# Weight products of the second expert stage moved from VectorE to GpSimd

## The chip, the cores and the metric

One NeuronCore of one Trainium2 chip runs the whole program. The metric is the device time of one execution in microseconds (us), the median of several runs. PE stands for TensorE, DVE for VectorE, ACT for ScalarE, POOL for GpSimd and SP for SyncE, the engine that issues most transfers. All data is float32; the large matrix products split each operand in a high part (fp32r) and a low remainder and use three matmuls.

## What is computed

The reference is one decoder layer for 512 tokens of width 2048: a combined projection, a gated convolution and differential attention, an output projection with layer norm, then a "product-key" expert layer, another norm and a gated embedding. Only the expert layer matters here:

```
q = (xb @ w_q).reshape(TOKEN_BLOCK, PEER_HEADS, 2, PEER_HALF)
s = einsum('thcd,hcnd->thcn', q, sub_keys)       # 128 keys per half, top 16 of each, top 16 of the sums
ids, g = ..., softmax(best)                      # 128 experts of 16384 per token
h = gelu(einsum('td,thkd->thk', xb, u_tab[ids]))
w = g * h
y = einsum('thk,thkd->td', w, v_tab[ids])        # x = LN(alpha * x + y)
```

## The kernel before

The tokens are split. For 352 tokens (`TU`) the expert layer is dense: the first expert stage computes gelu(u_tab x) for all 16384 experts, 128 units of 128 experts, and spills each 128x352 activation tile to HBM (`eg_sp[k, p, 0]`); the gates, summed per expert and token, are scattered into `eg_sp[k, p, 1]`, zero elsewhere. The second expert stage multiplies activation by gate and then by v_tab. The other 160 tokens are done sparsely: GpSimd gathers rows of u_tab and v_tab by indirect DMA (160 gathers of 128 rows of 2048 floats each, `NUP`), and VectorE does the dot products and, in the second stage, the weighted additions of rows.

The second expert stage is 16 groups of 8 K-chunks. In group g, TensorE runs 8 units u of two blocks each; a block is 8 chunks x 3 matmuls of 352 columns (`value_group`, L920, matmuls L651 to L653, called `three`). Its right-hand operands are the weights of the group: `xwhi[g % 2]` and `xwlo[g % 2]`, 8 tiles of 128x352 each, made one group ahead. Its left-hand operand is v_tab, streamed from HBM: SP loads `raw` (512 KB a block), ACT rounds it to `whi` (`hi_part`, L1019, L1025), and VectorE makes `wlo = raw - whi` (`lo_part`, L1575, L1578).

The weights of group g+1 are made during group g, tile k during unit k-1:

1. VectorE `weights_product` (L1651, instruction L1659): `wt = hg[.,0] * hg[.,1]`, activation times gate, 128x352. It waits for the transfer of `hg` (two chunks in 704 KB), and starts with a drain.
2. ACT `cast_weights` (L1234, L1237): `xwhi = fp32r(wt)`.
3. VectorE `weights_low` (L1661, L1664): `xwlo = wt - xwhi`.

VectorE's order in one unit (`add_values`, L1707) is: low part of tile u and product of tile u+1; wait for TensorE to have finished blocks 2u and 2u+1; add both banks to `res` (L1733 in group 0, L1735 after, 128x352 each, one input in PSUM); `lo_part` of block 2u+4; the gathered rows that fall in this unit (`add_early` L1683, `add_rows` L1675, instructions L1692, L1680: 128x2048, `y = row * w + y`, both tensors in SBUF); `lo_part` of block 2u+5. How many rows fall in a unit is written by hand in `V_ROWS`: group 0 has none, none, none, 1, 2, 2, 2, 2; group 1 has 1,1,1,2,1,2,1,2; groups 2, 3 and 14 have 1,2 four times; groups 4 to 13 have 1,1,1,2 twice; group 15 has 4 rows and no weights to make.

ACT's order in `value_steps` (L1239) is: `step(2u)`, which waits for block 2u and rounds the raw of block 2u+4; the cast of tile u+1; `step(2u+1)`, which rounds the raw of block 2u+5. So block 2u+5 is rounded after the cast, and the cast waits for the product of tile u+1:

```
for b in range(16):
    step(g * 16 + (B6 + b), b % 4)
    if b % 2 == 0 and not last:
        if b == 0: cast_weights(g + 1, 0, 1 - q)
        if b < 14: cast_weights(g + 1, b // 2 + 1, 1 - q)
```

SP's order in a group (`group_loads`, L510) is the raw of unit k, then, for odd k, a wait for the products up to tile k of the next group and the load of the `hg` pair that takes their place.

GpSimd, in this stage, only issues the row gathers (`gather_v`, L624, L631). There is a ring of 4 row buffers; gather n waits until VectorE has used row n-4. In the earlier part of the kernel (up to the first expert stage) and in its last part GpSimd makes the `wlo` instead of VectorE (L564, 128x1024); the same hardware pair can be seen at work there.

Of the kernel before, what the change touches and what calls it, by code (L numbers as in the profile page):

```python
# [19 lines left out]
F32 = mybir.dt.float32  # L20
F32R = mybir.dt.float32r
U32 = mybir.dt.uint32
ALU = mybir.AluOpType
# [33 lines left out]
B6 = B5 + 2 * U5  # L57
# [23 lines left out]
RING = 4  # L81

NXP = NP // NJ
NUP = NXP + NP


V_ROWS = [(0, 0, 0, 1, 2, 2, 2, 2), (1, 1, 1, 2, 1, 2, 1, 2), (1, 2, 1, 2, 1, 2, 1, 2), (1, 2, 1, 2, 1, 2, 1, 2),
          (1, 1, 1, 2, 1, 1, 1, 2), (1, 2, 1, 2, 1, 2, 1, 2), (1, 1, 1, 1, 0, 0, 0, 0)]
V_EARLY, V_LOOPED, V_EVE, V_LAST = 4, 4, 5, 6
# [3 lines left out]
V_START += [V_START[V_EVE] + sum(V_ROWS[V_EVE])]  # L93
assert V_START[V_LAST] + sum(V_ROWS[V_LAST]) == NUP
assert V_START[V_LOOPED] % 4 == 0 and 2 * V_PER % 4 == 0 and V_START[V_EARLY - 1] >= NXP
NTG = 24
TILE_DOTS = [j % 4 != 3 for j in range(32)]
POST_DOTS = [j % 5 != 4 and j < 20 for j in range(4 * (64 - POST))]
assert sum(TILE_DOTS) == NTG and NTG * NRT + sum(POST_DOTS) == NUP and NTG % RING == 0
assert NTG < NXP <= 2 * NTG  # L100

# [19 lines left out]
def build(nc, ws, xT, pT, cpar, pvec, lamT, keysT, u_tab, v_tab, out):  # L121
# [6 lines left out]
    with ExitStack() as ctx:  # L128
# [38 lines left out]
        xwhi = [at(f"xwhi{i}", o, [P, 8, TU], F32R) for i, o in enumerate((o_s, o_ahi))]  # L167
        xwlo = [at(f"xwlo{i}", o + 12 * KB, [P, 8, TU], F32R) for i, o in enumerate((o_s, o_ahi))]
# [7 lines left out]
        def small(name, shape, dt=F32):  # L176
            n = 4
            for s in shape[1:]:
                n *= s
            t = at(name, c[0], shape, dt)  # L180
            c[0] += (n + 31) // 32 * 32
            return t
# [113 lines left out]
        hg = small("hg", [P, 2, 2, 2, TU])  # L296
        wt = small("wt", [P, 2, TU])
# [30 lines left out]
        blk_done = sem("blk_done")  # L328
# [51 lines left out]
        hg_first = [sem(f"hg_first{i}") for i in range(2)]  # L380
        hg_in = [sem(f"hg_in{i}") for i in range(2)]
# [19 lines left out]
        wt_ok = sem("wt_ok")  # L401
        cast_ok = sem("cast_ok")
        w_ok = sem("w_ok")
# [136 lines left out]
        def _(pool):  # L540
# [80 lines left out]
                    pool.dma_start(hg[:, n % 2], eg_sp[2 * n:2 * n + 2].rearrange("k p c t -> p k c t")  # L621
                                   ).then_inc(hg_first[n % 2], 16)

            def gather_v():  # L624

                pool.wait_ge(blk_done, B6)
                for n in range(NUP):
                    if n >= RING:
                        pool.wait_ge(rows_used, NUP + n - RING + 1)
                    at_col = xg[:, 0, n:n + 1].bitcast(U32) if n < NXP else idx[:, n - NXP:n - NXP + 1]  # L630
                    nc.gpsimd.indirect_dma_start(  # L631
                        vrows[:, n % RING], None, v_tab,
                        bass.IndirectOffsetOnAxis(ap=at_col, axis=0)).then_inc(rows_in[n % RING], 16)
# [4 lines left out]
            pool.wait_ge(xg_in, 16 * NJ)  # L638
            gather_u()
            first_gates()  # L640
            gather_v()

            pool.wait_ge(lo_done, B7)
            lo_parts(B7, NB - B7)
# [673 lines left out]
        def _(dve):  # L1318
# [14 lines left out]
            for q in range(KD // 2):  # L1333
                k = slice(2 * q, 2 * q + 2)
# [209 lines left out]
            last = TT - 1  # L1544
# [64 lines left out]
            def expert_tile(t, extra=False):  # L1609
                n = 0  # L1610

                def next_dot():
                    nonlocal n
                    if extra and NTG * t + n < NXP:
                        extra_dot(NTG * t + n)
                    else:
                        dot(NTG * t + (n - NXP), NTG // RING * t + n // RING, n % RING)
                    n += 1
# [19 lines left out]
            for t in range(3, NRT):  # L1638
                expert_tile(t)
            n = NTG * NRT  # L1640
            for j, with_dot in enumerate(POST_DOTS):
# [6 lines left out]
            dve.drain().then_inc(dots_ok, 1)  # L1648


            def weights_product(g, k, ahead=False):  # L1651

                s = k // 2 % 2
                dve.drain()
                if ahead:
                    dve.wait_ge(hg_first[s], g * 32 + 16 * (k // 4 + 1))
                else:
                    dve.wait_ge(hg_in[s], g * 32 + 16 * (k // 4 - 2))
                dve.tensor_tensor(wt[:, k % 2], hg[:, s, k % 2, 0], hg[:, s, k % 2, 1], ALU.mult).then_inc(wt_ok, 1)  # L1659

            def weights_low(g, k, q):  # L1661

                dve.wait_ge(cast_ok, g * 8 + (k - 7))
                dve.tensor_tensor(xwlo[q][:, k], wt[:, k % 2], xwhi[q][:, k].bitcast(F32), ALU.subtract  # L1664
                                  ).then_inc(w_ok, 1)

            def weights_here(k):
                weights_product(0, k, ahead=True)
                dve.drain()
                dve.tensor_copy(xwhi[0][:, k], wt[:, k % 2])  # L1670
                dve.drain()
                dve.tensor_tensor(xwlo[0][:, k], wt[:, k % 2], xwhi[0][:, k].bitcast(F32), ALU.subtract
                                  ).then_inc(w_ok, 1)
# [33 lines left out]
            def add_values(g, q, kind, i=0):  # L1707
                first, eve, last = kind == 0, kind == V_EVE, kind == V_LAST
                if eve:
                    dve.wait_ge(yx_full, 1)  # L1710
                    r = res[:, :, TU:TD]
                    dve.scalar_tensor_tensor(r, r, ALPHA, quad[:, 0:KD * NX].rearrange("p (k t) -> p k t", k=KD),
                                             ALU.mult, ALU.add)
                    dve.drain().then_inc(yx_used, 1)
                for u in range(8):
                    ahead = not last or u < 6
                    if not last:

                        if u == 0:
                            weights_product(g + 1, 0, ahead=first)  # L1720
                        if u == 1:
                            weights_low(g + 1, 0, 1 - q)
                        if u >= 1:
                            weights_low(g + 1, u, 1 - q)
                        if u < 7:
                            weights_product(g + 1, u + 1, ahead=first and u < 3)
                    dve.wait_ge(blk_done, g * 16 + (B6 + 2 * u + 2))
                    for n in range(2):
                        r = res[:, 2 * u + n, 0:TU]
                        p = ps[2 * ((u + 1) % 2) + n][:, 0:TU]  # L1730
                        if first:

                            ad = dve.scalar_tensor_tensor(r, r, ALPHA, p, ALU.mult, ALU.add)  # L1733
                        else:
                            ad = dve.tensor_tensor(r, r, p, ALU.add)  # L1735
                    ad.then_inc(evac6, 1)
                    if ahead:
                        lo_part(g * 16 + (B6 + 2 * u + 4), 2 * u % 4)
                    if last:
                        for n in range(2):  # L1740
                            dve.drain()
                            if u == 0 and n == 0:
                                dve.tensor_copy(msum2[:, 0:TU], res[:, 0, 0:TU])
                            else:
                                dve.tensor_tensor(msum2[:, 0:TU], msum2[:, 0:TU], res[:, 2 * u + n, 0:TU], ALU.add)
                    start = V_START[kind] + sum(V_ROWS[kind][:u])
                    for r in range(start, start + V_ROWS[kind][u]):
                        if kind < V_EARLY:
                            add_early(r)
                        elif kind == V_LOOPED:  # L1750
                            r += q * V_PER
                            add_rows(2 * V_PER * i + r, V_PER // 2 * i + r // RING, r % RING)
                        else:
                            add_rows(r, r // RING, r % RING)
                    if last and u == 3:
                        dve.drain().then_inc(yacc_ok, 1)
                    if last and u == 4:
                        dve.wait_ge(p_in, 16)
                        dve.tensor_copy(phi[:], pin[:])
                        dve.drain()  # L1760
                        dve.tensor_tensor(plo[:], pin[:], phi[:].bitcast(F32), ALU.subtract).then_inc(p_ok, 1)
                    if last and u == 6:

                        dve.wait_ge(yacc_full, 1)
                        for n in range(4):
                            r = res[:, 4 * n:4 * n + 4, TD:T]
                            dve.scalar_tensor_tensor(r, r, ALPHA, ps[4 + n][:].rearrange("p (k t) -> p k t", k=4),
                                                     ALU.mult, ALU.add)
                        dve.drain().then_inc(yacc_used, 1)
                        dve.tensor_reduce(msum2[:, TU:T], res[:, :, TU:T].rearrange("p k t -> p t k"), AX.X, ALU.add)  # L1770
                    if ahead:
                        lo_part(g * 16 + (B6 + 2 * u + 5), (2 * u + 1) % 4)
# [79 lines left out]
```

## Time and profile before

| | |
|---|---|
| three runs | 3876.55, 3867.3, 3873.48 us |
| median | 3873.48 us |
| span of the profiled execution | 3703.5 us (its own device time is not listed beside it) |
| PE busy | 3634.4 us, 98% |
| DVE busy | 2612.3 us, 71% |
| ACT busy | 1289.2 us, 35% |
| POOL busy | 1692.4 us, 46% |
| second expert stage | from 2476 us to 3464 us of the span |

The span runs from the first to the last instruction; the device time has some 170 us more around it (3873.48 - 3703.5). Shares of busy time are means over stages that differ; the second expert stage is a quarter of the span, and is read by itself below. A "low part" below is an L1578 instruction, a "row" an L1680 or L1692 instruction.

### The profile page before, as it was taken

The numbers are of one execution on the slowest core, as the hardware profiler recorded it, in microseconds if no ns is written. First come the engines' busy times: TensorE is split into PE (matmuls) and PEld (weight loads), VectorE is DVE, ScalarE is ACT, GpSimd is POOL, SyncE is SP. The second block draws the span as 40 slices with busy tenths as digits, with TensorE's granted clock in tenths as the row PEclk, the third lists the DMA queues.
The fourth block names the chain that finished last, engine by engine and source line by source line (L and its number), as shares of the span: only waits on it lengthen the run. The fifth ranks groups of instructions, "written<-read, shape, count | busy, mean of one in ns | idle before, by whom it ended". The sixth has DMA issues, their size and how long they took to land.

```text
span 3703.5 us, 56572 instructions
## 1 busy us (share of the span) xinstructions
PE 3634.4 (98%) x19704; PEld 3304.0 (89%) x19704; DVE 2612.3 (71%) x4018; ACT 1289.2 (35%) x1659; POOL 1692.4 (46%) x1044
## 2 busy tenths in 40 slices
PE   8999999999999899999999999999999999999999
PEld 6888888877888688999999999989999999999777
DVE  3555555553431499987889888779999999999732
ACT  4334433343121523344433333323333333333532
POOL 4444444433444244668777776633332222222143
PEclk9999999999999999999999999999999999999999
DMA  5343333333443223478999999999999999999232
GB/s 182 128 131 125 130 125 130 128 106 117 151 135 124 77 87 101 158 274 304 340 369 376 367 372 363 325 340 352 381 372 356 358 359 352 361 357 343 86 117 76
DMA packets 245798, 873.52 MB, mean 236 GB/s; under 512 B 35600, under 2 KB 76752, under 8 KB 204624
## 3 DMA queue, kind: packets, MB, share of 16 engines
q1 hardware_dynamic: 154864, 496.64, 38.6%
q0 software_dynamic: 59360, 340.13, 23.9%
q10 hardware_dynamic: 31488, 35.66, 2.7%
q8 instruction: 47, 0.77, 0.1%
q14 instruction: 39, 0.32, 0.0%
HBM read 813.38 MB, written 58.90 MB: 236 GB/s over the span
## 4 chain that ended last, share of the span: by engine, by line
PE 63%; POOL 16%; DVE 10%; issue 5%; DMA 2%; DVEq 2%; ACT 1%; ACTq 0%; SPq 0%; POOLq 0%
PE bank L651 20%; PE bank L653 20%; PE bank L652 20%; POOL expert_spill L587 12%; POOL urows L605 4%; DVE hot L1524 1%; PE quad L694 1%; DMA expert_spill<-gval,goff 1%; DVE sc L1387 1%; PE bank L713 1%; DVE pick L1527 1%; DVE topi L1488 0%; DVE topi L1481 0%; DVE s4b L1482 0%; DMA urows<-u_tab,idx 0%
## 5 line engine op out<-in xcount | busy, mean ns | idle before, releaser
L1025 ACT ACTIVATE whi<-raw 128x1024 fp32r<-128x1024 f32 x784 | 827.9, 1059 | 1944.7 <-PE bank L653 1340.3
L651 PE MATMUL bank<-ahi,whi 128*128 128x352 f32 (+1 forms) x3968 | 1430.7, 361 | 44.0 <-DVE wlo L1578 22.7
L653 PE MATMUL bank<-ahi,wlo 128*128 128x352 f32 (+1 forms) x3968 | 1416.6, 357 | 0.0
L652 PE MATMUL bank<-alo,whi 128*128 128x352 f32 (+1 forms) x3968 | 1416.0, 357 | 0.0
L564 POOL TENSOR_TENSOR wlo<-raw,whi 128x1024 fp32r<-128x1024 f32 x316 | 787.7, 2496 | 1070.8 <-ACT whi L1025 1058.1
L651 PEld LDWEIGHTS bank<-ahi,whi 128*128 128x128 f32 x3968 | 750.7, 189 | 139.9 <-issue 30.9
L653 PEld LDWEIGHTS bank<-ahi,wlo 128*128 128x128 f32 x3968 | 750.8, 189 | 76.9
L652 PEld LDWEIGHTS bank<-alo,whi 128*128 128x128 f32 x3968 | 751.1, 189 | 72.3 <-issue 0.5
L651 PE MATMUL bank<-xwhi,whi 128*128 128x352 f32 x2048 | 662.7, 324 | 3.1 <-issue 1.7
L653 PE MATMUL bank<-xwhi,wlo 128*128 128x352 f32 x2048 | 658.6, 322 | 0.0
L652 PE MATMUL bank<-xwlo,whi 128*128 128x352 f32 x2048 | 658.0, 321 | 0.0
L1578 DVE TENSOR_TENSOR wlo<-raw,whi 128x1024 fp32r<-128x1024 f32 x472 | 575.6, 1220 | 18.3 <-ACT whi L1025 15.9
L587 POOL DMA_INDIRECT expert_spill<-gval,goff x384 | 449.1, 1170 | 145.6 <-issue 115.5
L631 POOL DMA_INDIRECT vrows<-v_tab,idx x128 | 207.0, 1617 | 547.6 <-DVE yacc L1680 492.0
L651 PEld LDWEIGHTS bank<-xwhi,whi 128*128 128x128 f32 x2048 | 385.4, 188 | 4.2 <-issue 1.9
L652 PEld LDWEIGHTS bank<-xwlo,whi 128*128 128x128 f32 x2048 | 386.6, 189 | 0.0
L653 PEld LDWEIGHTS bank<-xwhi,wlo 128*128 128x128 f32 x2048 | 385.0, 188 | 0.0
L1584 DVE SCALAR_TENSOR_TENSOR urows<-urows,quad 128x2048 f32<-128x2048 f32 x128 | 292.6, 2286 | 70.0 <-DMA urows<-u_tab,idx 69.0
L1680 DVE SCALAR_TENSOR_TENSOR yacc<-vrows,hd,yacc 128x2048 f32<-128x2048 f32 x116 | 273.4, 2357 | 24.9 <-issue 23.5
L1387 DVE SCALAR_TENSOR_TENSOR sc<-glu,cur,sc 128x512 f32<-128x512 f32 x232 | 270.2, 1165 | 17.3
L1237 ACT ACTIVATE xwhi<-wt 128x352 fp32r<-128x352 f32 x120 | 59.8, 498 | 345.0 <-DVE wt L1659 343.1
L1353 DVE RECIPROCAL rcp<-sums 128x2 f32<-128x2 f32 x32 | 5.3, 166 | 230.8 <-ACTq L1084 230.8
(229 smaller groups left out, 2787.8 us busy)
## 6 DMA issues: line engine op xcount, KB each, us to landing
raw<-ws SPq DMA_DIRECT2D x788, 512.0 KB
hg<-expert_spill SPq DMA_DIRECT2D x58, 704.0 KB, 9.1
expert_spill<-zero SPq DMA_DIRECT2D x32, 704.0 KB, 5.9
expert_spill<-hst ACTq DMA_DIRECT2D x128, 176.0 KB
gate_spill<-gout ACTq DMA_DIRECT2D x32, 256.0 KB, 2.0
gl<-gate_spill SPq DMA_DIRECT2D x32, 256.0 KB, 2.7
expert_spill<-gval,goff POOLq DMA_INDIRECT x384
hg<-expert_spill POOLq DMA_DIRECT2D x6, 704.0 KB, 6.1
```

What stands on the lines that cost most here:

```text
L564: nc.gpsimd.tensor_tensor(wlo[:, s], raw[:, s // 2, s % 2], whi[:, s].bitcast(F32), ALU.subtract).then_inc(lo_done, 1)
L587: nc.gpsimd.indirect_dma_start(eg_flat, bass.IndirectOffsetOnAxis(ap=goff[here, a, n:n + 1], axis=0), gval[here, a, n:n + 1], None).then_i ...
L605: nc.gpsimd.indirect_dma_start(urows[:, n % RING], None, u_tab, bass.IndirectOffsetOnAxis(ap=at_col, axis=0)).then_inc(rows_in[n % RING], 16)
L631: nc.gpsimd.indirect_dma_start(vrows[:, n % RING], None, v_tab, bass.IndirectOffsetOnAxis(ap=at_col, axis=0)).then_inc(rows_in[n % RING], 16)
L651: pe.matmul(ps_out, hi, xh, start=first, stop=False)
L652: pe.matmul(ps_out, hi, xl, start=False, stop=False)
L653: return pe.matmul(ps_out, lo, xh, start=False, stop=last)
L1025: act.activation(whi[:, s], raw[:, s // 2, s % 2], ACT.Copy).then_inc(hi_done, 1)
L1387: dve.scalar_tensor_tensor(dst, glu[:, w:w + T], cur[:, w:w + 1], acc, ALU.mult, ALU.add)
L1578: dve.tensor_tensor(wlo[:, s], raw[:, s // 2, s % 2], whi[:, s].bitcast(F32), ALU.subtract).then_inc(lo_done, 1)
L1584: dve.scalar_tensor_tensor(urows[:, s], urows[:, s], 1.0, quad[:], ALU.mult, ALU.mult, accum_out=hd[:, bass.ds(n, 1)]).then_inc(rows_used, 1)
L1680: dve.scalar_tensor_tensor(yacc[:], vrows[:, s], w, yacc[:], ALU.mult, ALU.add).then_inc(rows_used, 1)
```

## The change

GpSimd makes the products and their low halves for groups 1 to 15 (120 products and 120 low parts of 128x352). For group 0 VectorE still makes them, as before (`weights_here`). GpSimd's `gather_v` is cut in pieces: the first four gathers, and then for each unit those gathers whose buffer is freed by a row of that unit. Ahead of each piece come the low part of tile u and the product of tile u+1 of the next group. ACT's casts and SP's loads keep their order and their waits.

```diff
@@ gpsimd
-            def gather_v():
-                pool.wait_ge(blk_done, B6)
+            def weights_product(g, k):
+                s = k // 2 % 2
+                pool.drain()
+                if g == 1 and k < 4:
+                    pool.wait_ge(hg_first[s], g * 32 + 16 * (k // 4 + 1))
+                else:
+                    pool.wait_ge(hg_in[s], g * 32 + 16 * (k // 4 - 2))
+                nc.gpsimd.tensor_tensor(wt[:, k % 2], hg[:, s, k % 2, 0], hg[:, s, k % 2, 1], ALU.mult
+                                        ).then_inc(wt_ok, 1)
+            def weights_low(g, k):
+                pool.wait_ge(cast_ok, g * 8 + (k - 7))
+                nc.gpsimd.tensor_tensor(xwlo[g % 2][:, k], wt[:, k % 2], xwhi[g % 2][:, k].bitcast(F32),
+                                        ALU.subtract).then_inc(w_ok, 1)
+            def gather_v(unit):
                 for n in range(NUP):
+                    if n >= RING and ROW_UNIT[n - RING] != unit or n < RING and unit >= 0:
+                        continue
                     if n >= RING:
                         pool.wait_ge(rows_used, NUP + n - RING + 1)
...
-            gather_v()
+            pool.wait_ge(blk_done, B6)
+            gather_v(-1)
+            pool.wait_ge(w_ok, 8)
+            for g in range(16):
+                for u in range(8):
+                    if g < 15:
+                        if u == 0:
+                            weights_product(g + 1, 0)
+                        if u == 1:
+                            weights_low(g + 1, 0)
+                        if u >= 1:
+                            weights_low(g + 1, u)
+                        if u < 7:
+                            weights_product(g + 1, u + 1)
+                    gather_v(8 * g + u)
@@ vector, add_values
-                    if not last:
-                        if u == 0:
-                            weights_product(g + 1, 0, ahead=first)
-                        if u == 1:
-                            weights_low(g + 1, 0, 1 - q)
-                        if u >= 1:
-                            weights_low(g + 1, u, 1 - q)
-                        if u < 7:
-                            weights_product(g + 1, u + 1, ahead=first and u < 3)
                     dve.wait_ge(blk_done, g * 16 + (B6 + 2 * u + 2))
```

## Rows read from the trace of the kernel before

**Rows 1.** Windows: time, then busy us (and instructions) of each engine, clock, DMA
```profile
2602.00:2662.00 60.00, 60.00 (x374) 60.00 (x374) 58.25 (x59) 19.34 (x24) 23.37 (x12) 1.00 0.98 383
2980.00:3040.00 60.00, 60.00 (x379) 60.00 (x378) 55.50 (x58) 19.91 (x24) 14.63 (x10) 1.00 0.96 358
```

**Rows 2.** Waits of PE in the second expert stage, 2476 to 3464 us
```profile
PE bank L651 <- issue: 1.7, 1, 1.7
PE bank L651 <- DVE xwlo L1664: 0.6, 1, 0.6
```

**Rows 3.** Chain of waits, start us, us, what; second expert stage, its longest pieces
```profile
2542.59 0.43 PE bank L651
2725.19 3.49 PE quad L949 x32
2729.53 0.29 PE bank L652
```

**Rows 4.** Lines of DVE from 2476 to 3464 us, busy, mean ns, idle before
```profile
L1659 DVE TENSOR_TENSOR wt<-hg 128x352 f32<-128x352 f32 x122 | 64.1, 525 | 13.0 <-issue 3.7
L1664 DVE TENSOR_TENSOR xwlo<-wt,xwhi 128x352 fp32r<-128x352 f32 x120 | 61.0, 519 | 0.0
L1733 DVE SCALAR_TENSOR_TENSOR res<-res,bank 128x352 f32<-128x352 f32 x16 | 7.6, 517 | 9.5 <-PE bank L653 9.5
```

**Rows 5.** Timeline of DVE, start us and duration, one unit with one row
```profile
2869.45 0.94 DVE L1735 TENSOR_TENSOR res<-res,bank 128x352 f32<-128x352 f32 x2
2870.31 1.22 DVE L1578 TENSOR_TENSOR wlo<-raw,whi 128x1024 fp32r<-128x1024 f32 x1
2871.74 2.35 DVE L1680 SCALAR_TENSOR_TENSOR yacc<-vrows,hd,yacc 128x2048 f32<-128x2048 f32 x1 [0.21 <-issue]
2874.01 1.22 DVE L1578 TENSOR_TENSOR wlo<-raw,whi 128x1024 fp32r<-128x1024 f32 x1
2875.14 0.52 DVE L1664 TENSOR_TENSOR xwlo<-wt,xwhi 128x352 fp32r<-128x352 f32 x1
2875.75 0.53 DVE L1659 TENSOR_TENSOR wt<-hg 128x352 f32<-128x352 f32 x1
2876.20 0.95 DVE L1735 TENSOR_TENSOR res<-res,bank 128x352 f32<-128x352 f32 x2
```

**Rows 6.** Timeline of DVE, two rows in one unit (x2)
```profile
2544.98 4.80 DVE L1692 SCALAR_TENSOR_TENSOR yx<-vrows,hx,yx 128x2048 f32<-128x2048 f32 x2 [0.45 <-issue]
```

**Rows 7.** Timeline of POOL: gathers in a unit with one row, then with two
```profile
2874.36 1.68 POOL L631 DMA_INDIRECT vrows<-v_tab,idx  x1 [5.50 <-DVE yacc L1680]
...
2547.60 3.00 POOL L631 DMA_INDIRECT vrows<-v_tab,xg  x1 [4.26 <-DVE yx L1692]
2550.90 0.94 POOL L631 DMA_INDIRECT vrows<-v_tab,xg  x1 [0.30 <-issue]
```

**Rows 8.** Line L564 up to 1620 us: POOL's own subtraction, min/median/max ns
```profile
L564 POOL TENSOR_TENSOR wlo<-raw,whi x280: 2346/2401/3217, 7.6 to 1595.2; 128x1024 fp32r<-128x1024 f32 x140
```

**Rows 9.** Line L1387 of DVE, two SBUF inputs: min/median/max ns; one POOL instruction beside it
```profile
L1387 DVE SCALAR_TENSOR_TENSOR sc<-glu,cur,sc x232: 750/752/2834, 92.9 to 795.2; 128x512 f32<-128x512 f32 x116
...
308.57 2.40 POOL L564 TENSOR_TENSOR wlo<-raw,whi 128x1024 fp32r<-128x1024 f32 x1 [2.92 <-ACT whi L1025]
308.76 2.76 DVE L1387 SCALAR_TENSOR_TENSOR sc<-glu,cur,sc 128x512 f32<-128x512 f32 x1
```

**Rows 10.** Timeline at 1308 us: DVE with one SBUF input beside a POOL subtraction
```profile
1308.09 2.40 POOL L564 TENSOR_TENSOR wlo<-raw,whi 128x1024 fp32r<-128x1024 f32 x1 [3.98 <-ACT whi L1025]
...
1308.51 0.42 DVE L1481 FIND_INDEX8 pnow<-bnow,cand 128x8 uint32<-128x256 f32 x1
```

**Rows 11.** Timeline of ACT around 2876 us
```profile
2876.31 0.50 ACT L1237 ACTIVATE xwhi<-wt 128x352 fp32r<-128x352 f32 x1 [2.75 <-DVE wt L1659]
2876.72 1.04 ACT L1025 ACTIVATE whi<-raw 128x1024 fp32r<-128x1024 f32 x1
```

**Rows 12.** Waits of the SP queue, 2740 to 3360 us: us in total, times, longest
```profile
SPq L500 <- DVE wt L1659: 23.0, 40, 1.6
```

More of the change, by code:

```diff
@@ L95 @@
 assert V_START[V_LOOPED] % 4 == 0 and 2 * V_PER % 4 == 0 and V_START[V_EARLY - 1] >= NXP
+V_UNITS = [V_ROWS[g] if g < V_LOOPED else V_ROWS[V_LOOPED] for g in range(14)] + [V_ROWS[V_EVE], V_ROWS[V_LAST]]
+ROW_UNIT = [8 * g + u for g in range(16) for u in range(8) for _ in range(V_UNITS[g][u])]
+assert len(ROW_UNIT) == NUP
 NTG = 24
@@ L1648, in _, with weights_here @@
             dve.drain().then_inc(dots_ok, 1)
-            def weights_product(g, k, ahead=False):
+            def weights_here(k):
                 s = k // 2 % 2
                 dve.drain()
[L1655 to L1658, printed above, removed]
+                dve.wait_ge(hg_first[s], 16 * (k // 4 + 1))
                 dve.tensor_tensor(wt[:, k % 2], hg[:, s, k % 2, 0], hg[:, s, k % 2, 1], ALU.mult).then_inc(wt_ok, 1)
[L1661 to L1668, printed above, removed]
                 dve.drain()
```

## The prediction

> **What bounds the kernel now.** I read the page first: PE is busy 98% of the span. Then the windows of the second expert stage [rows 1]: PE is busy all of the 60 us, in groups 1 to 3 (first row) as in the looped groups (second row). The counts of the second row give the pace: 379 matmuls less the one that straddles the edge, so 60 / 378 = 0.159 us a matmul, 3.81 us a block of 24, 7.62 us a unit of two blocks. The waits of PE say how much the change could give [rows 2]: 0.6 us on a low half of the weights, in a stage of 988 us; the chain shows the place, 2542.59 us, the start of group 1 [rows 3]. The pace in groups 1 to 3 is 374 instead of 379 matmuls in 60 us, 1.3%, over 180 us some 2.4 us. That VectorE's load causes it is not shown; if it does, the most to be had is 0.6 + 2.4, say 3 us, under 0.1%. The second bound lies close behind: DVE is busy 58.25 of 60 us in groups 1 to 3 and 55.50 in the loop [rows 1]. So the question is not what PE gains, but whether DVE stays ahead of PE.
>
> **What is removed.** From DVE, 120 products of 0.525 us and 120 low parts of 0.519 us [rows 4], 125 us. A unit with one row takes 2876.20 - 2869.45 = 6.75 us, and 2875.14 - 2869.45 = 5.69 us of it is without the weights [rows 5]: 1.06 us a unit go. A second row adds 2.45 us [rows 6]. Without the weights a one-row unit takes 5.69 us and a two-row unit 8.14 us; the loop (six and two in a group) means 6.30 us, groups with 1,2,1,2 mean 6.92 us. Against 7.62 us both are faster than PE, if nothing is added.
>
> **What is added on POOL.** Its subtraction of 1024 columns takes 2.40 us [rows 8]; in proportion 352 columns take 0.83 us, an estimate without the fixed part of an instruction. Two of these and 1.25 gathers of 1.68 to 3.00 us [rows 7] are at most 5.4 us in a unit of 7.62: POOL has the time, and its own busy time costs nothing. What costs is where its work falls, in two ways.
>
> **First term: VectorE and GpSimd exclude each other.** Ahead of the first stage a DVE instruction with two inputs in SBUF takes 0.75 us, but 2.76 us when it begins 0.19 us after a POOL subtraction of 2.40 us [rows 9]: it is held up 2.01 us, so POOL holds it off for 2.20 of its 2.40 us. An instruction with one input in SBUF, beside the same POOL instruction, keeps its 0.42 us [rows 10]. In the second stage the low parts and the rows have two SBUF inputs, and the bank additions one. The POOL instruction of 0.83 us would hold off a low part or a row by up to 0.83 - 0.20 = 0.63 us (an estimate), and in turn waits for one that runs. Two of them, 1.26 us, are more than the 1.06 us that were removed. The Trainium skill, page SBUF — State Buffer, section Who interferes with whom, says that a VectorE instruction with two SBUF inputs and a GpSimd instruction that reads SBUF exclude each other, the later one blocked until the earlier is through. By the whole instruction, 0.83 us, one hold-off in each of the 117 units with rows would be 0.20 us longer, and the sum 23 us higher, 3945 us; this trace has 2.20 of 2.40, and the sum goes by the trace.
>
> **Second term: the order on POOL and ACT.** I walk one unit, W = 0 at its first bank addition, with DVE late (not waiting for PE). From [rows 5]: first low part 0.86 to 2.08, row 2.29 to 4.64, second low part to 5.77, next W at 5.69. The gather behind a row starts 0.27 us after the row and takes 1.68 [rows 7]; with 0.30 of issue, POOL asks for its low half 2.25 us after the row's end, which is W + 1.20. The first low part is already running since 0.86. So:
> - Late case: POOL's low half runs 2.08 to 2.91, the row ends at 5.06, and the product, asked for meanwhile, runs 5.06 to 5.89. The cast waits for the product, and block 2u+5 is rounded behind the cast: 1.48 us from the product's end to the end of that rounding [rows 5, 11]. The second low part begins at 7.42; next W at 8.55.
> - Early case (the low half was made under the bank additions): product 2.08 to 2.91, row to 5.06, next W at 6.11.
> After a late unit the gather ends some 7.1 us after W and the low half comes under the next bank additions, so that the next unit is an early one; after an early or a two-row unit a late one follows (the second gather of a pair ends 2.06 us after the second row [rows 6, 7], so the low half is asked for at W + 1.31). A two-row unit in the early case takes 6.11 + 2.45 = 8.56 us; in the late case the product holds the second row off for 0.54 more, 9.1 us.
>
> **The sum.** Loop, rows 1,1,1,2: 8.55 + 6.11 + 8.55 + 8.56 = 31.77 against 4 x 7.62 = 30.48 us, 1.29 us in four units, 20 times: 26 us. Pairs 1,2: 17.11 against 15.24, 1.87 us; groups 2, 3 and 14 have four, 22.4 us; group 1 has 1.29 + 2 x 1.87 = 5 us. Group 0 with its four two-row units: 0.94 + 3 x 1.48 = 5.4 us. Together 59 us. Off go two credits: in group 0 DVE waited 9.5 us for PE [rows 4], a lead of which I take half, 5 us; and PE's pause of 3.49 us with 12 matmuls at half its clock behind it, 0.29 instead of 0.16 us each (one of them stands in [rows 3]), 5 us in which DVE catches up. 49 us remain. Against the span of 3703.5 us that is 3752.5; its own device time is not shown, so I add it to the median: 3873.5 + 49 = **3922 us**.
>
> **Bounds of this.** Below: if POOL's instructions always find the gap, every unit is an early one (6.11 and 8.56, means 6.72 and 7.34, both under 7.62), and the cost is none, the gain up to 3 us. Above: every unit is a late one: the loop 6 x 8.55 + 2 x 9.1 = 69.5 against 61 us, 85 us in ten groups; groups 2, 3 and 14 9.6 us each, group 1 9, group 0 5; less 10: 118 us. I take the walk between them, since it follows the instants of the rows.
>
> **Edits that I cost at nothing.** The first four gathers stay where they were; the first two products come behind them, some 4 x 1.68 = 6.7 us later, and with them ACT's rounding of block 5. PE needs block 5 five blocks, 19 us, after the stage's start, and tile 0 of group 1 after 61 us; both hide it. The added drains on POOL have nothing but the previous low half to wait for. SP waits for the odd products before the hg load and has the next raw load behind it: before, 23 us in 40 waits, 0.6 each [rows 12]. Where the product comes at 5.89, and the first low part is done by 2.08, the raw load starts 3.8 us later; I add nothing, since four raw buffers stand ahead of that load, and keep it for the upper end.
>
> **Rivals.**
> 1. Not slower: the DVE time freed makes it wait for PE, W comes later against the gather, POOL's low half falls into that wait and the product costs 0.42 us (5.06 - 4.64). It decides at 0.35 us of wait in a one-row unit (1.20 - 0.86). For it: the DVE is then under PE's 7.62 us everywhere. Against it: every two-row unit (8.56) costs the wait again, and groups 1 to 3 begin with DVE late. 3870 to 3881 us. Chance 0.24.
> 2. Only the hold-offs, and no late rounding: 1.26 - 1.06 = 0.20 us a unit more than before where DVE was saturated (32 units), 6 us, and part of the loop: 3881 to 3898 us. Chance 0.13.
> 3. Much slower: all late, raw loads held behind SP's wait, and PE's clock at the lower level after each long stall, as at 2729 us [rows 3] (1.6 us each time): above 3963 us, up to 3991. Chance 0.15.
> 4. Faster by more than 8 us: nothing in PE's waits holds that much; 0.03.
> The forecast, 3898 to 3963 us, has 0.45.
>
> **Numbers.** A measurement of this kernel can tell about 0.2% (8 us) from no change. Slower is 0.45 + 0.13 + 0.15 = 0.73, same 0.24, faster 0.03. The range of 8 in 10 takes in rival 1 nearly whole and most of rival 3: 3868 to 3985 us; the forecast's own range is 3898 to 3963.
>
> **What would show it.** DVE's low parts and rows longer than 1.22 and 2.35 us on the mean, by about 0.6 us where a POOL instruction lies ahead; L1578 waiting for ACT's whi, and PE waiting for DVE's wlo, in groups 1 to 3 above all; products of POOL beginning at the end of a row rather than ahead of it; PE's pace in the loop above 7.62 us a unit. I am wrong in the mechanism if rows and low parts keep their lengths; wrong in the size, if PE still shows no waits in the loop, where the first term alone is too small. A POOL instruction of 352 columns far from 0.83 us would move both terms.

## The result, and the profile after

The changed kernel takes 4188.6 us (median of 4 runs, 4182 to 4199), the kernel before 3875.0 us beside it (4 runs, 3867 to 3887): a ratio of 1.081, 95% interval 1.079 to 1.084. That is 314 us slower. The forecast was slower, by 49 us, with a range up to 3985 us; the time lies 204 us above that range.

The first look is at the page, the chain of waits by engine, and a window of 600 us from the looped groups of the second expert stage (for the kernel before, see the looped row of [rows 1]).

```profile
PE 3813.8 (91%) x19704; PEld 3417.6 (81%) x19704; DVE 2555.1 (61%) x3778; ACT 1274.5 (30%) x1659; POOL 1887.5 (45%) x1284
...
PE 52%; issue 21%; POOL 11%; DVE 9%; POOLq 3%; DVEq 2%; ACT 1%; DMA 1%; ACTq 0%; SPq 0%
...
3060.00:3660.00 600.00, 505.84 (x2875) 489.87 (x2874) 395.75 (x315) 143.98 (x179) 223.15 (x193) 0.93 0.74 271
```

PE was busy for all of a 60 us window in the looped groups; now it is busy 506 of 600 us, and that time holds only 2875 matmuls, 0.176 us each instead of 0.159, at a granted clock of 0.93 instead of 1.00. But DVE is not what is full in its place: 396 of 600 us, 66%, where [rows 1] had 55.50 of 60. Nor is POOL, with 223 of 600. Every engine waits, which is the look of a chain of waits and not of a bound engine. The waits of the same stretch name its links:

```profile
ACT xwhi L1272 <- POOL wt L635: 415.0, 59, 11.2
POOL wt L635 <- issue: 305.5, 59, 7.5
DVE wlo L1613 <- ACT whi L1060: 188.6, 51, 7.3
PE bank L686 <- DVE wlo L1613: 93.8, 46, 6.5
```

From the bottom up: PE waits for VectorE's low parts, these for ACT's rounding, ACT's cast for POOL's product (L635), and the product for "issue", for nothing that the profile counts as work. 305.5 us in 59 times are 5.2 us each. What stands on POOL's queue there is the drain ahead of the product, L630 (minimum, median and maximum in ns), and the timeline of POOL in two units shows where it lies:

```profile
L630 POOLq DRAIN  x120: 1027/8260/19903, 2651.7 to 3883.7; - x120
```

```profile
2966.57 0.97 POOL L652 DMA_INDIRECT vrows<-v_tab,idx  x1
2967.84 0.94 POOL L652 DMA_INDIRECT vrows<-v_tab,idx  x1 [0.30 <-issue]
2968.79 1.18 POOL L641 TENSOR_TENSOR xwlo<-wt,xwhi 128x352 fp32r<-128x352 f32 x1
2975.95 0.94 POOL L635 TENSOR_TENSOR wt<-hg 128x352 f32<-128x352 f32 x1 [5.98 <-issue]
2977.05 0.96 POOL L652 DMA_INDIRECT vrows<-v_tab,idx  x1 [0.16 <-issue]
2978.02 0.94 POOL L641 TENSOR_TENSOR xwlo<-wt,xwhi 128x352 fp32r<-128x352 f32 x1
```

The low half ends at 2969.97 and the product begins at 2975.95. Between them POOL does nothing but drain. The drain's own record is longer, 8.26 us in the median, since it begins on the queue while the gather and the low half ahead of it still run; what it adds in idle time of POOL is the 5.2 us. The prediction had it at nothing.

One thing did not fit. The profiled span is 494 us longer than that of the kernel before (4197.3 - 3703.5), and the median time only 314 us. The windows of the first expert stage, which the change doesn't touch, from its first block to the first of the second stage, before and after:

```profile
1451.00:2476.00 1025.00, 1000.62 (x6180) 994.74 (x6179) 863.75 (x1578) 367.81 (x424) 729.85 (x590) 0.99 0.87 319
```

```profile
1448.00:2647.00 1199.00, 1083.50 (x6179) 1039.35 (x6178) 865.90 (x1580) 365.44 (x422) 723.98 (x590) 0.93 0.78 273
```

The first stage is 174 us longer, at 273 instead of 319 GB/s. The kernel before has 170 us between its listed times (3873) and its span (3703.5), while the changed kernel's own device time, 4199.2 us, is its span and 2 us. So the profile of before seems to be of an execution some 170 us faster than the runs listed beside it. The experiments below take that up.

### The profile page after: what moved, and what is told of

Its sections match the earlier page's. It is cut to its first block, busy times and chain, and to the rows that moved or that the text cites. A ratio compares the mean times of both kernels' runs of the same rounds, so it can differ in the third digit from the quotient of the medians.

```text
span 4197.3 us, 56477 instructions
## 1 busy us (share of the span) xinstructions
PE 3813.8 (91%) x19704; PEld 3417.6 (81%) x19704; DVE 2555.1 (61%) x3778; ACT 1274.5 (30%) x1659; POOL 1887.5 (45%) x1284
## 4 chain that ended last, share of the span: by engine, by line
PE 52%; issue 21%; POOL 11%; DVE 9%; POOLq 3%; DVEq 2%; ACT 1%; DMA 1%; ACTq 0%; SPq 0%
PE bank L686 16%; PE bank L688 16%; PE bank L687 16%; POOL wt L635 4%; POOLq L630 3%; POOL vrows L652 3%; POOL expert_spill L590 2%; DVE hot L1559 1%; POOL xwlo L641 1%; PE quad L729 1%; POOL urows L608 1%; DVE sc L1422 1%; DVE wlo L1613 1%; PE bank L748 1%; DVE yacc L1702 1%
## 5 line engine op out<-in xcount | busy, mean ns | idle before, releaser
L1613 DVE TENSOR_TENSOR wlo<-raw,whi 128x1024 fp32r<-128x1024 f32 x472 | 623.6, 1322 | 665.3 <-ACT whi L1060 584.8
L686 PE MATMUL bank<-xwhi,whi 128*128 128x352 f32 x2048 | 706.9, 345 | 223.7 <-DVE wlo L1613 209.5
L687 PE MATMUL bank<-xwlo,whi 128*128 128x352 f32 x2048 | 689.2, 337 | 0.0
L688 PE MATMUL bank<-xwhi,wlo 128*128 128x352 f32 x2048 | 688.4, 336 | 0.0
L686 PEld LDWEIGHTS bank<-xwhi,whi 128*128 128x128 f32 x2048 | 411.5, 201 | 253.3 <-DVE wlo L1613 235.3
L590 POOL DMA_INDIRECT expert_spill<-gval,goff x384 | 420.8, 1096 | 141.1 <-issue 115.5
L635 POOL TENSOR_TENSOR wt<-hg 128x352 f32<-128x352 f32 x120 | 175.2, 1460 | 644.1 <-issue 644.1
L687 PEld LDWEIGHTS bank<-xwlo,whi 128*128 128x128 f32 x2048 | 413.1, 202 | 0.0
L688 PEld LDWEIGHTS bank<-xwhi,wlo 128*128 128x128 f32 x2048 | 411.3, 201 | 0.0
L608 POOL DMA_INDIRECT urows<-u_tab,idx x128 | 157.0, 1227 | 218.6 <-DVE urows L1619 186.2
```

The lines of the kernel that those rows point to most:

```text
L590: nc.gpsimd.indirect_dma_start(eg_flat, bass.IndirectOffsetOnAxis(ap=goff[here, a, n:n + 1], axis=0), gval[here, a, n:n + 1], None).then_i ...
L608: nc.gpsimd.indirect_dma_start(urows[:, n % RING], None, u_tab, bass.IndirectOffsetOnAxis(ap=at_col, axis=0)).then_inc(rows_in[n % RING], 16)
L635: nc.gpsimd.tensor_tensor(wt[:, k % 2], hg[:, s, k % 2, 0], hg[:, s, k % 2, 1], ALU.mult).then_inc(wt_ok, 1)
L686: pe.matmul(ps_out, hi, xh, start=first, stop=False)
L687: pe.matmul(ps_out, hi, xl, start=False, stop=False)
L688: return pe.matmul(ps_out, lo, xh, start=False, stop=last)
```

## The experiments

All other comparisons ran beside runs of the kernel before of 3708 or 3709 us in the median, not 3873. "The drainless kernel" below is the change with its drain replaced as in the first experiment. Stage times below are from the first matmul of the stage to the first one behind it. In the profile of before the second expert stage takes 988.2 us, and a looped group 61.0 us (median).

**A semaphore in place of the drain.** The drain guards one thing: the product overwrites a buffer that the low half two tiles earlier has read. A wait for the count of finished low halves does the same.

```diff
@@ gpsimd, weights_product
-                pool.drain()
+                pool.wait_ge(w_ok, g * 8 + k - 1)
```

> The changed kernel with the one drain ahead of each GpSimd product replaced by a wait for the count of finished low halves (the reader of the buffer that the product overwrites). Everything else stays. Theory A (the drain waits for the row gathers in flight, 7 us and more a unit, and ACT's cast and rounding wait behind it): nearly all of the 313 us go; what is left is what GpSimd's work costs by itself. Theory B (mutual exclusion of VectorE and GpSimd and the late rounding, the two terms of the prediction, are the main cost): the time stays above 4100 us. If A holds, this run also measures the prediction's two terms: 3898 to 3963 us if they were right, under 3885 us if GpSimd's instructions find the gaps.

3776.6 us against 3708.8, ratio 1.018 (1.016 to 1.020): 68 us over the kernel before. The second stage takes 1058 us. Theory A stands, and the run also measures what the prediction had costed: 68 us where 49 stood.

**The drains alone.** The products and low halves stay on VectorE.

```diff
@@ gpsimd, on the kernel before (gather_v is cut in pieces as in the change)
-            gather_v()
+            pool.wait_ge(blk_done, B6)
+            gather_v(-1)
+            pool.wait_ge(w_ok, 8)
+            for g in range(16):
+                for u in range(8):
+                    if g < 15:
+                        if u == 0:
+                            pool.drain()
+                        if u < 7:
+                            pool.drain()
+                    gather_v(8 * g + u)
```

> The kernel before, with its products and low halves on VectorE, the gathers cut in the same pieces as in the change, and one GpSimd drain where the change has one, with nothing of the weights on GpSimd. Theory A: each drain takes about as long as in the change (5 to 10 us behind a gather, 1 us where none is in flight), the gathers come at most once in some 9.5 us, VectorE waits for rows, and the time is 4050 to 4250 us. Theory B: drains have nothing to wait for, within 10 us of the kernel before.

3901.8 us, one run: 193 us over the kernel before, with none of the weights' arithmetic on GpSimd. The 105 drains of units 0 to 6 (in unit 0 the second one) have a median like the change's (ns); the short ones, 34 to 53 ns, come right behind another drain. The 15 first drains of unit 0 are not in the line; their median is 15.99 us.

```profile
L654 POOLq DRAIN  x105: 34/8159/12242, 2503.8 to 3594.5; - x105
```

The expectation was 4050 to 4250 us on a base of 3873; on this base that is 3885 to 4085, and the run lies at its lower end. Here the rows come late and VectorE waits for them, and ACT's cast waits for VectorE's product (469.4 us in 72 times from 2740 to 3500 us) and not for one of GpSimd.

**The change again, on the same base.**

> The changed kernel as it is, so that it stands on the same chip as the experiments. In the first comparison the kernel before took 3873 us, beside the experiments it took 3709 us, and its profile spanned 3703.5 us. The first expert stage, which the change does not touch, took 1199 us in the profile of the changed kernel and 1025 us in that of the kernel before. If that is the chip or its memory and not the change, the first stage takes about 1027 us here too, and the time is 3709 + 196 (drains alone) + 68 (without drains) = 3973 us or up to 60 more if the two add to more than their sum (the second stage took 1312 us in the profile against 988). If the change itself slows the first stage, it takes some 1199 us here and the time is above 4150 us.

4030.7 us against 3707.7, ratio 1.086 (1.083 to 1.090), 323 us slower. The first stage takes 1024 us, as in the kernel before: what was 174 us longer in the first comparison is not the change. The second takes 1316 us, as in the first profile of the change (1312). So the second stage holds the whole cost, 328 us of it. The parts, 193 and 68 us, make 261; 62 us more are left. That they come from both standing in one line (the drain, the product behind it and the gather behind that are in series) is argued, and no run shows it. The window of the stage shows in what form PE pays:

```profile
2473.00:3789.00 1316.00, 1088.12 (x6193) 1058.72 (x6193) 850.78 (x699) 305.23 (x376) 477.41 (x404) 0.92 0.72 263
```

PE is idle for 228 us of it, where it was idle for 2 us before; and its matmuls, as many as before, take 1088 us instead of 986, with the granted clock at 0.92 instead of 1.00. So about 226 us of the 328 are idle time and 102 us are slower matmuls.

**Short rows.** The change, with a quarter of the bytes in each gather. It leaves out three quarters of each row, so its result is not that of the kernel.

```diff
@@ gpsimd, gather_v
-                        vrows[:, n % RING], None, v_tab,
+                        vrows[:, n % RING, 0:512], None, v_tab.rearrange("e (q d) -> (e q) d", q=4),
@@ gpsimd
+            nc.gpsimd.memset(vrows[:], 0.0)
+            pool.drain()
             gather_v(-1)
```

> The change with its drains, but each gather of values brings 512 columns a row (from another place of the table) instead of 2048; the rest of each row buffer is set to zero once, and the values of the last 160 tokens are left wrong by that. As many rows and descriptors, a quarter of the bytes. If the drain waits for the landing of the gathers in flight, the drains behind one gather fall from some 8 us to 3.5 to 5.5 us, and the second stage to 1030 to 1130 us. If it waits for GpSimd's own making of the descriptors, they keep their 8 us and the stage its length.

3841.1 us, one run; the second stage takes 1122 us. The drains, first of the change again, then with short rows:

```profile
L630 POOLq DRAIN  x120: 1025/8257/19727, 2478.1 to 3713.9; - x120
```

```profile
L630 POOLq DRAIN  x120: 1031/5236/7505, 2493.4 to 3529.8; - x120
```

A gather still has 128 rows, and the median drain falls from 8.26 to 5.24 us. But not only the bytes fall: the trace has 64 packets of 4 KB a gather here, and 128 of 8 KB in the change, so this run alone doesn't tell the bytes from the count of packets. The times of the packets say it more sharply. Between 2700 and 3700 us of the span I took each drain of over 2 us and the last packet of the last gather issued before its end: the drain ends 0.42 us (median; 0.37 to 0.58) behind that packet's end in the change, 0.47 (0.36 to 0.57) with short rows, and 0.43 (0.36 to 0.67) in the kernel with the drains alone, 253 drains in all. In these kernels a GpSimd drain waits until the row gathers that GpSimd has issued have landed.

**Only the products, and only the low halves.** Both without the drain: the product waits for the count of finished low halves, on VectorE too in the second kernel.

```diff
@@ gpsimd, only the products            @@ gpsimd, only the low halves
-  weights_low(g + 1, 0)                -  weights_product(g + 1, 0)
-  weights_low(g + 1, u)                -  weights_product(g + 1, u + 1)
@@ vector, add_values (as before)       @@ vector, add_values (as before)
+  weights_low(g + 1, 0, 1 - q)         +  weights_product(g + 1, 0, ahead=first)
+  weights_low(g + 1, u, 1 - q)         +  weights_product(g + 1, u + 1, ahead=first and u < 3)
```

> Without the drain, only the products on GpSimd, the low halves back on VectorE. The product is the part on which ACT's cast and the rounding of block 2u+5 wait. If the prediction's second term (late product, late rounding) is what remains without the drain, this has most of what the drainless kernel has over the kernel before; if the exclusion by count of instructions is, about half of it. If nothing remains in the drainless kernel, it is within 8 us of the kernel before.

> Without the drain, only the low halves on GpSimd, the products back on VectorE. Nothing of ACT waits on GpSimd here. By the second term nothing remains: within 8 us of the kernel before. By the exclusion alone, 0.63 us lost for 0.52 removed a unit, also within 8 us, perhaps 10 slower.

Products only: 3713.6 us, ratio 1.0013 (1.0002 to 1.0023), 5 us slower. Low halves only: 3717.6 us, ratio 1.0027 (1.0011 to 1.0043), 9 us slower. Together they cost 68. So neither the product's place in ACT's order nor a cost in proportion to the count of instructions explains it, and the next two runs go at the order itself.

**The order of ACT, and of POOL.**

```diff
@@ scalar, value_steps
-                    if b % 2 == 0 and not last:
+                    if b % 2 == 1 and not last:
-                        if b == 0:
+                        if b == 1:
                             cast_weights(g + 1, 0, 1 - q)
-                        if b < 14:
+                        if b < 15:
                             cast_weights(g + 1, b // 2 + 1, 1 - q)
```

> Without the drain, and with ACT's cast of tile u+1 placed behind step(2u+1) instead of behind step(2u), so that the rounding of block 2u+5 does not wait for the product. If the late rounding (second term) makes the 68 us that the drainless kernel has over the kernel before, at most 15 us of them stay: by the walk 6.11 to 6.85 us a one-row unit and 8.56 a two-row unit, 3705 to 3725 us. If the exclusion is the cause, over 40 us of the 68 stay.

3772.4 us, ratio 1.017 (1.014 to 1.020): 65 us over the kernel before, so of the 68 us nearly all stay. The late rounding is not the cause.

```diff
@@ gpsimd
                        if u == 1:
                            weights_low(g + 1, 0)
+                       if u < 7:
+                           weights_product(g + 1, u + 1)
                        if u >= 1:
                            weights_low(g + 1, u)
-                       if u < 7:
-                           weights_product(g + 1, u + 1)
```

> Without the drain, with GpSimd making the product of tile u+1 ahead of the low half of tile u, so that the product comes 0.95 us earlier and is never pushed behind the row. Both instructions still exclude VectorE. If the late product is the cause, the time falls to 3705 to 3725 us; if the exclusion is, it stays within 15 us of the drainless kernel's 3777 us.

3764.3 us, ratio 1.015 (1.012 to 1.018), 57 us slower, 12 us under the drainless kernel. The exclusion is left. These are VectorE's lines in the drainless kernel, 2740 to 3400 us:

```profile
L1613 DVE TENSOR_TENSOR wlo<-raw,whi 128x1024 fp32r<-128x1024 f32 x162 | 340.8, 2104 | 2.3 <-ACT whi L1060 2.3
L1702 DVE SCALAR_TENSOR_TENSOR yacc<-vrows,hd,yacc 128x2048 f32<-128x2048 f32 x97 | 229.1, 2362 | 22.9 <-issue 22.9
L1747 DVE TENSOR_TENSOR res<-res,bank 128x352 f32<-128x352 f32 x162 | 76.4, 513 | 0.0
```

A low part took 1.22 us in [rows 5] and takes 2.10 us on the mean now; the rows keep their 2.36 us, and the bank additions wait for PE no more. Where the time goes, the timelines of POOL and of DVE show:

```profile
2963.65 1.71 POOL L652 DMA_INDIRECT vrows<-v_tab,idx  x1 [3.92 <-DVE yacc L1702]
2965.38 1.86 POOL L641 TENSOR_TENSOR xwlo<-wt,xwhi 128x352 fp32r<-128x352 f32 x2
2967.21 0.93 POOL L635 TENSOR_TENSOR wt<-hg 128x352 f32<-128x352 f32 x1
```

```profile
2964.43 0.94 DVE L1747 TENSOR_TENSOR res<-res,bank 128x352 f32<-128x352 f32 x2
2965.29 3.93 DVE L1613 TENSOR_TENSOR wlo<-raw,whi 128x1024 fp32r<-128x1024 f32 x1
2969.43 2.35 DVE L1702 SCALAR_TENSOR_TENSOR yacc<-vrows,hd,yacc 128x2048 f32<-128x2048 f32 x1 [0.20 <-issue]
```

The gather ends just as VectorE's bank additions do (2965.36 and 2965.37), and POOL's instructions, back to back, then get through ahead of the first low part: here three (tile 0 and 1 of a group's beginning), 3.93 us for 1.22, otherwise mostly two. The low part does not get in between them, although its record begins 0.09 us ahead of POOL's first. Over the 660 us, 81 low parts lie beside POOL's arithmetic and 81 do not: these keep a median of 1.22 us, and the others take 2.12 us beside one instruction (12 times), 3.02 beside two (59) and 3.93 beside three (10), 0.90 us for each.

For products only, the same line over the same stretch shows what a single instruction does:

```profile
L1603 DVE TENSOR_TENSOR wlo<-raw,whi 128x1024 fp32r<-128x1024 f32 x171 | 240.9, 1409 | 0.0
```

0.19 us more a low part, 0.38 a unit, since only 37 of POOL's 81 us in this stretch lie beside low parts; 35 lie beside the bank additions, which have one SBUF input and keep their 0.515 us. In the drainless kernel it is 0.885 a low part, 1.77 us a unit: 150 of POOL's 154 us lie beside low parts. Against the 1.06 us removed [rows 5] a single one is a loss of nothing (0.38 for 0.52), and two are a loss of 0.71 us a unit. VectorE had less than that to spare in the loop: 6.75 us a one-row unit and 9.20 a two-row unit mean 7.36 against PE's 7.62.

**Writes only.** GpSimd's instructions stay in number, place and semaphores, but read nothing; the weights of groups 1 to 15 are not computed. The fills are also shorter, 0.41 us instead of 0.95.

```diff
@@ gpsimd, weights_product and weights_low of the drainless kernel
-                nc.gpsimd.tensor_tensor(wt[:, k % 2], hg[:, s, k % 2, 0], hg[:, s, k % 2, 1], ALU.mult
-                                        ).then_inc(wt_ok, 1)
+                nc.gpsimd.memset(wt[:, k % 2], 0.01).then_inc(wt_ok, 1)
...
-                nc.gpsimd.tensor_tensor(xwlo[g % 2][:, k], wt[:, k % 2], xwhi[g % 2][:, k].bitcast(F32),
-                                        ALU.subtract).then_inc(w_ok, 1)
+                nc.gpsimd.memset(xwlo[g % 2][:, k].bitcast(F32), 0.0).then_inc(w_ok, 1)
```

> The drainless kernel, with each of GpSimd's products and low halves replaced by a fill of the same 128x352 tile with a constant, which reads nothing from SBUF (so the weights of groups 1 to 15 are not computed). Same count, same places, same semaphores; the fill of 352 columns took 0.39 us at the kernel's start, the product 0.95. If VectorE is held off because GpSimd reads SBUF, its low parts keep their 1.22 us and a looped group takes 61 to 62 us. If any GpSimd instruction beside it holds it off, the low parts grow by up to 0.8 us a unit (0.4 each on the mean), still within what VectorE has, so that it is the length of the low parts and not the time that tells.

3700.2 us, one run, beside one of 3709.3 of the kernel before. The lines of DVE and POOL, 2740 to 3400 us:

```profile
L1611 DVE TENSOR_TENSOR wlo<-raw,whi 128x1024 fp32r<-128x1024 f32 x174 | 211.7, 1217 | 0.0
...
L1745 DVE TENSOR_TENSOR res<-res,bank 128x352 f32<-128x352 f32 x174 | 82.6, 515 | 100.8 <-PE bank L686 100.7
```

```profile
L640 POOL MEMSET xwlo<- 128x352 f32 x88 | 35.0, 407 | 0.1
L635 POOL MEMSET wt<- 128x352 f32 x86 | 34.3, 408 | 0.0
```

The low parts are back at 1.217 us, and VectorE waits 101 us for PE. Most of the 174 fills lie beside bank additions or idle time and test nothing, but 47 of them ran wholly within a low part (24 low parts), and those took 1.21 us too. One of them, VectorE and then GpSimd:

```profile
2949.88 1.21 DVE L1611 TENSOR_TENSOR wlo<-raw,whi 128x1024 fp32r<-128x1024 f32 x1
...
2949.90 0.41 POOL L640 MEMSET xwlo<- 128x352 f32 x1
2950.23 0.41 POOL L635 MEMSET wt<- 128x352 f32 x1
```

It is GpSimd's reading that holds VectorE off. The Trainium skill, page SBUF — State Buffer, section Who interferes with whom, says that a GpSimd instruction which only writes doesn't contend with a VectorE instruction of two SBUF inputs; this run agrees, and so do the 2.10 us of the drainless kernel with what it says of one that reads. This kernel is also the bound of what the move could have given, since here VectorE is rid of the work at no price: the second stage takes 984.5 us against 988.2, 3.7 us.

## Why the prediction was wrong

**The limit of the gain was right.** The prediction had "say 3 us" as the most to be had; the kernel with the work gone and no price gains 3.7 us in the stage.

**The step that failed is the drain.** "The added drains on POOL have nothing but the previous low half to wait for." They wait for the landing of the row gathers: of 120 drains 102 take over 2 us, and the median of all is 8.26 us. The gather was in the trace with its landing, 6.2 to 10.4 us after issue, and each product was put behind one; what a drain on a queue with transfers in flight does was not in any row, and the term should have been bounded from both sides, above by that landing, and not set at nothing. A one-row unit then is drain, product, gather, landing in series, 9.80 us in the change again (2969.17 to 2978.97 from product to product), against the 7.62 of PE:

```profile
2969.17 0.95 POOL L635 TENSOR_TENSOR wt<-hg 128x352 f32<-128x352 f32 x1 [7.13 <-issue]
2970.27 0.96 POOL L652 DMA_INDIRECT vrows<-v_tab,idx  x1
2971.25 0.94 POOL L641 TENSOR_TENSOR xwlo<-wt,xwhi 128x352 fp32r<-128x352 f32 x1
2978.97 0.95 POOL L635 TENSOR_TENSOR wt<-hg 128x352 f32<-128x352 f32 x1 [6.78 <-issue]
```

Over 112 units 2.2 us each would be 244 us, and units with two rows take one gather more. Replacing the drain takes away 254 of the 323 us (4030.7 to 3776.6 us).

**The first term, exclusion, was right in kind and too small.** It was set at 0.63 us for a POOL instruction and found to be 0.885 on the mean of all units, 0.90 for each that lies beside a low part. A POOL instruction of 352 columns takes 0.95 us, not the 0.83 of proportion: (2.40 - 0.95) / 672 columns is 2.16 ns a column, which leaves 0.19 us that don't depend on the columns. And its place was off: I let 0.30 us of issue pass between gather and low half, so that VectorE's low part came first; it is 0.02 us (2965.36 to 2965.38), and POOL gets through first. The walk also let a row be held off, but the rows kept their 2.36 us: it is the first low part that pays. By rows it is then 1.77 - 1.06 = 0.71 us a unit more than VectorE had before; by the 7.36 us above that is 8.07 us a unit, 64.6 us a group. The looped groups took 65.5 us (median) instead of 61.0.

**The second term, the late rounding, was wrong.** It would have been gone with ACT's other order, and 65 us of the 68 stayed. In the drainless kernel the product comes ahead of the row, not behind it. That the walk's 49 us came near the 68 is luck, two errors against each other.

**The rivals.** Without the drain the kernel is the second rival in kind, only the hold-offs and no late rounding; that rival's cost, up to 25 us, was too small. The third, much slower, had raw loads and PE's clock for its causes. The granted clock was at the lower level for 207 us of the second stage in the change again, against 3 us before, and in the drainless kernel for only 24: it follows the long waits. 161 us of PE's busy time lie at that level, and by the 0.29 us of a matmul there against 0.16 some 70 of the 102 us of slower matmuls are the clock's, an estimate. What the 328 us would have been at the full clock is open, since PE would have waited longer for POOL where it was faster; the 254 us of the drain's replacement hold the clock's part with the rest.

**The base.** The median was taken from listed runs of 3873 us and the sums from a span of 3703.5; the difference was called time around the span. It is 2 us. The change's first profile has the rest in the first stage (1199 against 1025 us, 273 against 319 GB/s), and the kernel before seems to have had it too: the change costs 314 us on the one base and 323 on the other. Why the first stage was slower there, by the chip, its memory or something else, is not shown; no trace of the kernel before at 3873 us is at hand.

## What to carry to other kernels

A GpSimd drain behind gathers that GpSimd issued is a wait for their landing; where it guards a buffer, a wait on the reader's semaphore can take its place, and here it brought back 254 us. Work moved to GpSimd is not free for VectorE if it reads SBUF: one instruction a unit, partly beside VectorE's PSUM additions, cost 5 or 9 us in all, two back to back took more than they relieved. And no relief of VectorE could have paid here, since PE had some 3 us to gain in the stage; no version tried that keeps the computation beats the kernel before.

## What the runs showed of the hardware that was not expected

- A GpSimd drain ended 0.42 to 0.47 us (medians) behind the last packet of the gathers in flight in three kernels (253 drains, none outside 0.36 to 0.67). With no gather in flight it took 1.02 to 1.51 us behind GpSimd's arithmetic, mostly the 0.95 us of the instruction ahead of it, and 0.03 to 0.05 behind another drain.
- GpSimd kept VectorE off over a run of instructions: a low part of 1.22 us lasted 2.12, 3.02 and 3.93 us beside one, two and three of them.
- PE's pace differs a little with no wait that the profile shows: a looped group takes 61.0 us in the kernel before and with writes only, 61.4 with the low halves on GpSimd, 61.9 with the products there. Its cause stays open, as for the 1.3% of groups 1 to 3 in [rows 1]; with writes only and VectorE relieved, groups 1 and 2 take 61.4 us, where they took 62.9 and 61.9.
